# Recurrent down products one tile later, key-stage panels in halves, first queries loaded back early

## The reference

```python
# layer 0: gated recurrent mixer, 1536 channels
u = hn @ w_in; xb, yb = u[..., :1536], u[..., 1536:]
xc = causal_conv4(xb) + conv_b
r, i = sigmoid(blocks(xc, w_ra) + b_ra), sigmoid(blocks(xc, w_ix) + b_ix)
a = exp(-8 * r * softplus(-lam))
hs = scan(h_t = a_t * h_{t-1} + sqrt(1 - a_t**2) * i_t * xc_t)
h = h + (hs * gelu(yb)) @ w_out
# ... a gated feed-forward layer, then keys and values shared by the attention layer:
kv = rmsnorm(h) @ kv_w      # compressed, selected and window keys and values, 4 groups
kc, vc = gelu(windows(k_cmp) @ w1k) @ w2k, gelu(windows(v_cmp) @ w1v) @ w2v
# layer 1: 16 heads, three branches (compressed, selected, window), summed with gates
q = (hn @ w_q) * 96**-0.5   # 16 x 96, unrotated for kc, rotated for the other two
out = g0 * attend(q, kc, vc) + g1 * attend(rope(q), ks, vs) + g2 * attend(rope(q), kw, vw)
```

## Time and profile before

| | us |
|---|---|
| median of three runs (2611.04 to 2611.66) | 2611.09 |
| the profiled execution, its own time | 2616.25 |
| its span, first to last instruction | 2614.4 |
| TensorE busy in the span | 2440.1 |

### The profile page before, as it was taken

How to read it: one execution, slowest core, us unless ns; L and a number is a source line. 1 busy time by engine, 2 the same in 40 slices (tenths; PEclk the granted TensorE clock), 3 DMA queues, 4 the chain that set the end, 5 groups by cost and what they waited for, 6 DMA issues and landing times.

```text
span 2614.4 us, 28494 instructions
## 1 busy us (share of the span) xinstructions
PE 2440.1 (93%) x10912; PEld 1899.6 (73%) x10912; DVE 1406.2 (54%) x1711; ACT 1075.9 (41%) x1324; POOL 165.9 (6%) x140
## 2 busy tenths in 40 slices
PE   5999799999999979999999999899999889999958
PEld 4777678888778758887788888677787666666646
DVE  4666554444566645553544444556533556666654
ACT  3444443333333324452433333344422346666622
POOL 0333300000000000000000000300000000000020
PEclk9999899999999989999999999899999799999978
DMA  3222122222133431001222222011221239999941
GB/s 146 89 89 89 57 97 96 96 96 96 37 129 115 156 102 31 26 25 43 105 96 96 96 96 80 33 65 49 97 97 65 97 121 391 397 393 400 372 161 49
DMA packets 55808, 324.79 MB, mean 124 GB/s; under 512 B 6208, under 2 KB 6336, under 8 KB 25632
## 3 DMA queue, kind: packets, MB, share of 16 engines
q1 hardware_dynamic: 49072, 300.44, 30.5%
q0 software_dynamic: 5664, 20.84, 2.6%
q10 hardware_dynamic: 976, 2.21, 0.2%
HBM read 294.63 MB, written 28.84 MB: 124 GB/s over the span
## 4 chain that ended last, share of the span: by engine, by line
PE 83%; DVE 9%; ACT 3%; issue 2%; POOL 2%; DMA 1%; ACTq 0%; SPq 0%; POOLq 0%; DVEq 0%
PE psum L527 21%; PE psum L528 21%; PE psum L529 21%; PE psum L1159 5%; PE psum L899 3%; PE psum L846 3%; DVE a_lo L1695 2%; PE psum L863 1%; DVE tmp L1745 1%; PE psum L1121 1%; ACT a_hi L1204 1%; DVE hn_lo L1739 1%; PE psum L896 1%; PE psum L611 1%; DVE hs L1794 1%
## 5 line engine op out<-in xcount | busy, mean ns | idle before, releaser
L527 PE MATMUL psum<-hn_hi,a_hi 128*128 128x512 f32 (+2 forms) x1584 | 640.2, 404 | 33.9 <-DVE hn_lo L1739 20.0
L528 PE MATMUL psum<-hn_lo,a_hi 128*128 128x512 f32 (+2 forms) x1584 | 634.9, 401 | 0.0
L529 PE MATMUL psum<-hn_hi,a_lo 128*128 128x512 f32 (+2 forms) x1584 | 632.9, 400 | 0.0
L527 PEld LDWEIGHTS psum<-hn_hi,a_hi 128*128 128x128 f32 (+2 forms) x1584 | 299.4, 189 | 125.3 <-issue 23.4
L529 PEld LDWEIGHTS psum<-hn_hi,a_lo 128*128 128x128 f32 (+2 forms) x1584 | 298.9, 189 | 76.3 <-issue 0.8
L528 PEld LDWEIGHTS psum<-hn_lo,a_hi 128*128 128x128 f32 (+2 forms) x1584 | 299.6, 189 | 73.7 <-issue 1.0
L1695 DVE TENSOR_TENSOR a_lo<-a_raw,a_hi 128x2048 fp32r<-128x2048 f32 x117 | 271.1, 2318 | 113.4 <-ACT a_hi L1204 113.2
L1204 ACT ACTIVATE a_hi<-a_raw 128x2048 fp32r<-128x2048 f32 x117 | 223.1, 1908 | 134.7 <-PE psum L529 127.5
L2312 DVE TENSOR_TENSOR moe_lo<-moe_raw,moe_hi 128x2048 fp32r<-128x2048 f32 x78 | 178.7, 2292 | 43.7 <-ACT moe_hi L1622 43.3
L1781 DVE TENSOR_TENSOR h<-h,psum 128x512 f32<-128x512 f32 x176 | 121.1, 688 | 93.1 <-PE psum L529 91.6
L1622 ACT ACTIVATE moe_hi<-moe_raw 128x2048 fp32r<-128x2048 f32 x78 | 149.0, 1912 | 43.5 <-PE psum L529 26.5
(11 more groups left out here) (427 smaller groups left out, 3669.4 us busy)
## 6 DMA issues: line engine op xcount, KB each, us to landing
a_raw<-w_a SPq DMA_DIRECT2D x117, 1024.0 KB, 5.2
moe_raw<-w_m SPq DMA_DIRECT2D x78, 1024.0 KB, 9.0
moe_down<-w_m SPq DMA_DIRECT2D x39, 1024.0 KB, 8.3
b_raw<-w_b SPq DMA_DIRECT2D x64, 512.0 KB, 3.3
expert_out<-y_out SPq DMA_DIRECT2D x39, 512.0 KB, 8.5
q_scratch<-qb POOLq DMA_DIRECT2D x8, 768.0 KB, 5.3
qs<-q_scratch POOLq DMA_DIRECT2D x16, 384.0 KB, 3.6
out_t<-h POOLq DMA_DIRECT2D x8, 256.0 KB, 2.3
```

The lines of the kernel that those rows point to most:

```text
L527: pe.matmul(out, w_hi, x_hi, start=first, stop=False)
L528: pe.matmul(out, w_hi, x_lo, start=False, stop=False)
L529: return pe.matmul(out, w_lo, x_hi, start=False, stop=last)
```

## The change

Three places of the program change; no product is added or taken away.

1. In the recurrent layer, TensorE makes the tile `branch(g, 1, 0, ...)` ahead of `rnn_down(g - 1, 0)` rather than behind it. VectorE makes the low part of the gates' panel and the third convolution (with its `xc_lo`) ahead of `add_rnn(g - 1, 0)`, and ScalarE the third `high_xc` ahead of `high_b(B_RNN + 3g - 1)`.
2. The five panels of `HALVES` are rounded and split in two halves of 1024 columns; TensorE begins on the first half (`half_ready`) and waits for the whole panel ahead of the fifth of its eight slices. VectorE takes `low_a(A_W1V + 1)` ahead of four copies of values.
3. GpSimd loads heads 0 and 1 back when pair 1 has been stored, between the stores; ahead of head 2 it waits for all stores. `pt`, `pm` and `ptc` move over the b-buffers, so that `qs` no longer lies over `qb`. TensorE no longer waits for all rotations ahead of attention, and VectorE rotates the last pair behind `peak(0)`.

```diff
+HALVES = [A_K + 2, A_K + 4, A_K + 6, A_VCMP, A_W1V + 1]
...
             xv_lo = sb("xv_lo", [P, CSTRIDE, GROUPS * NCMP], F32R, st)
+        with ExitStack() as st:
+            sb("under_attention", [P, 3 * 2 * WA], F32, st)
+            pt = sb("pt", [P, 2, 2, S], F32, st)
+            pm = sb("pm", [P, 2, 2, S], F32, st)
+            ptc = sb("ptc", [NCMP, 2, S], F32, st)
...
             with ExitStack() as s2:
-                pt = sb("pt", [P, 2, 2, S], F32, s2)
-                ptc = sb("ptc", [NCMP, 2, S], F32, s2)
...
                 ob = sb("ob", [P, 2, 3, DV], F32, s2)
-                sb("under_pm", [P, P], F32, s2)
-                pm = sb("pm", [P, 2, 2, S], F32, s2)
+                sb("under_staged", [P, 7 * S], F32, s2)
...
+            def whole(s, n):
+                if s in HALVES:
+                    pe.wait_ge(half_ready, HALVES.index(s) + 1)
+                else:
+                    pe.wait_ge(a_ready, n + 1)
+            def rest(s, n, k):
+                if s in HALVES and k == KT // 2:
+                    pe.wait_ge(a_ready, n + 1)
...
                 n = s + 2 * i
-                pe.wait_ge(a_ready, n + 1)
+                whole(s, n)
+                def hh_rest(k):
+                    rest(s, n, k)
+                    return hh(k)
...
                     b = tile_bank(s, j, n)
-                    product(b[0:width, :], s, j * width, 2 * width, width, hh, hl).then_inc(tile_ready, 1)
+                    product(b[0:width, :], s, j * width, 2 * width, width, hh if j else hh_rest, hl) \
+                        .then_inc(tile_ready, 1)
...
                 branch(g, 0, 1, 1, f + 1)
+                branch(g, 1, 0, 2, f + 2)
...
                     rnn_down(g - 1, 0)
-                branch(g, 1, 0, 2, f + 2)
...
-            pe.wait_ge(rope_done, 8 + HEADS)
-            pe.wait_ge(tile_free, 2 * A_WO)
+            pe.wait_ge(rope_done, 8)
...
             scores_c(0)
+            pe.wait_ge(tile_free, 2 * A_WO)
...
                     act.wait_ge(tile_ready, 2 * n - 2)
-                act.activation(a_hi[s % 2][:, :], a_raw[s % 2][:, :], ACT.Copy).then_inc(a_rounded, 1)
+                if s in HALVES:
+                    act.activation(a_hi[s % 2][:, 0:WB], a_raw[s % 2][:, 0:WB], ACT.Copy).then_inc(half_rounded, 1)
+                    act.activation(a_hi[s % 2][:, WB:WA], a_raw[s % 2][:, WB:WA], ACT.Copy).then_inc(a_rounded, 1)
+                else:
+                    act.activation(a_hi[s % 2][:, :], a_raw[s % 2][:, :], ACT.Copy).then_inc(a_rounded, 1)
...
                     high_a(A_RNN + 4 * g + 2)
+                    high_xc(g, 2)
...
                 if g < RNN_GROUPS:
-                    high_xc(g, 2)
...
             expo(0)
-            for u in range(2):
-                act.wait_ge(q_stored[u], 16 * (HEADS // 4))
...
                 n = s + 2 * i
+                if s in HALVES:
+                    V.wait_ge(half_rounded, HALVES.index(s) + 1)
+                    V.tensor_tensor(a_lo[s % 2][:, 0:WB], a_raw[s % 2][:, 0:WB], a_hi[s % 2][:, 0:WB], ALU.subtract) \
+                     .then_inc(half_ready, 1)
+                    V.wait_ge(a_rounded, n + 1)
+                    V.tensor_tensor(a_lo[s % 2][:, WB:WA], a_raw[s % 2][:, WB:WA], a_hi[s % 2][:, WB:WA], ALU.subtract) \
+                     .then_inc(a_ready, 1)
+                    return
...
                     low_xc(g, 1)
-                if g:
-                    add_rnn(g - 1, 0)
-                if g < RNN_GROUPS:
                     low_a(A_RNN + 4 * g + 2)
-                if g:
-                    low_b(B_RNN + 3 * g - 1)
-                if g < RNN_GROUPS:
...
                 if g:
+                    add_rnn(g - 1, 0)
+                    low_b(B_RNN + 3 * g - 1)
...
             normalise(N_MIX1, 3)
+            low_a(A_W1V + 1)
...
             ins.then_inc(tile_free, 6)
-            low_a(A_W1V + 1)
...
             V.sem_inc(tile_free, 2)
+            def rotate_q(p):
+                for j in range(2):
+                    v = 2 * (p % 2) + j
+                    V.wait_ge(base_ready, 8 + 2 * p + j + 1)
+                    step(V.tensor_tensor(sq[0:ROT, j, :], qb[0:ROT, v, 0, :], cs[0:ROT, :], ALU.mult))
+                    V.wait_ge(tile_free, 2 * (A_Q + p) + j + 1)
+                    V.wait_ge(base_copied, 2 * p + j + 1)
+                    V.tensor_tensor(qb[0:ROT, v, 1, :], tmp[0:ROT, j, :], sq[0:ROT, j, :], ALU.add).then_inc(rope_done, 1)
...
                                            ALU.mult, ALU.mult).then_inc(tile_free, 1)
-                for j in range(2):
-                    v = 2 * (p % 2) + j
-                    V.wait_ge(base_ready, 8 + 2 * p + j + 1)
-                    step(V.tensor_tensor(sq[0:ROT, j, :], qb[0:ROT, v, 0, :], cs[0:ROT, :], ALU.mult))
-                    V.wait_ge(tile_free, 2 * s + j + 1)
-                    V.wait_ge(base_copied, 2 * p + j + 1)
-                    V.tensor_tensor(qb[0:ROT, v, 1, :], tmp[0:ROT, j, :], sq[0:ROT, j, :], ALU.add).then_inc(rope_done, 1)
+                if p < HEADS // 2 - 1:
+                    rotate_q(p)
...
                 V.wait_ge(o_ready, 3 * hd + 1 + 2 * half)
+                if hd == 0 and half == 0:
+                    for u in range(2):
+                        V.wait_ge(q_stored[u], 16 * (HEADS // 4))
...
             peak(0)
+            rotate_q(HEADS // 2 - 1)
...
                 store_q(p)
-            pool.wait_ge(q_stored[0], 16 * (HEADS // 4))
-            stage_q(0)
-            stage_q(1)
-            pool.wait_ge(q_stored[1], 16 * (HEADS // 4))
+                if p == 1:
+                    pool.wait_ge(q_stored[0], 16)
+                    pool.wait_ge(cmp_w2, 2)
+                    stage_q(0)
+                    stage_q(1)
+            for u in range(2):
+                pool.wait_ge(q_stored[u], 16 * (HEADS // 4))
```

More of the change, by code:

```diff
@@ L350, in build @@
             sem("m2_done"), sem("mult_done"), sem("bx_done"), sem("scan_done"), sem("rec_done"))
+        half_rounded, half_ready = sem("half_rounded"), sem("half_ready")
         base_ready, base_copied, rope_done = sem("base_ready"), sem("base_copied"), sem("rope_done")
@@ L750, in compress_v @@
                 s = A_W1V + p
-                pe.wait_ge(a_ready, s + 1)
+                whole(s, s)
                 if p == 0:
@@ L754, in compress_v @@
                 for l in range(8):
+                    rest(s, s, l)
                     t = 8 * p + l
```

## The result

| | before | after |
|---|---|---|
| median of four runs, us | 2611.07 (2610.36 to 2611.66) | 2567.49 (2566.72 to 2577.95) |
| the profiled execution, us | 2616.25 | 2567.22 |
| its span, us | 2614.4 | 2565.2 |

The ratio is 0.9843, with a 95% interval of 0.9817 to 0.9868: 43.6 us less. The forecast was 2568, in a range of 2562 to 2583.

The account below looks back on a forecast made before the run. TensorE, busy 93% of the span, bounds the kernel; time is won where it idles or runs at the lower clock. 11.8 + 5.2 + 6.3 + 2.9 + 2.1 + 12.0 + 3.0 = 43.3 us off 2611.09 gives 2568 us, range 2562 to 2583.

Parts of the forecast that it names:

- 11.8 of waits: Recurrent layer: the moved tile covers three of TensorE's four waits for the low part of `rhid`, 11.8 us.
- 5.2 of clock: Recurrent layer: the low clock behind the `rhid` waits goes with them, 5.2 us at most, nothing at least.
- what is late next: Recurrent layer, second down products: first addition and b-panel come 2.3 and 1.8 us early, so no new wait appears.
- Forecast 11.3 us: Panel halves: 6.3 us of four key-stage waits, 2.9 of low clock, 2.1 of the wait ahead of `compress_v(1)`.
- about 2.4 us were to stay: Ahead of `compress_v(1)`: the first half is ready 2.1 us sooner, and some 2.4 us of the wait stay.
- The allowance of 1.2 us: Halves: VectorE's queued copies may delay the first half, 0.3 us a panel, 1.2 in all, allowed in the range.
- The price of nothing for a wait within a product: Five split panels: a wait in the middle of a product costs nothing; otherwise the sum would be 0.9 us smaller.
- the row of FFN 0: FFN 0: one panel of two has a wait ahead of every slice, yet matmuls average 0.233 us.
- The 12.0 us of the wait: Start of attention: with heads 0 and 1 loaded after pair 1, `scores_c(0)` starts 12.0 us earlier.
- I take 3.0: First head of attention: full clock wins up to 7.6 us, less 4.2 of exposed VectorE work; 3.0 us taken.
- the clock falls in the ramp: Rival, start of attention: short waits lower the clock; queries give 7.8 instead of 15, total 32, 2579 us; chance 0.14.

Follow-up runs that it names:

- the last kernel: Changed kernel with the last pair's rotation behind `peak(1)` and the first group's panel 1 rounded and split ahead of the group loop: 2564.36 us, ratio 0.9813.
- TensorE's order alone: Kernel before with only TensorE's moved `branch(g, 1, 0, ...)` tile, VectorE and ScalarE as before: 2596.62 us, one execution.
- a wait in every slice: Changed kernel with a TensorE wait for a long-raised semaphore ahead of every triple of matmuls: 2569.0 us, one execution.
- the rotation last: Changed kernel with the last pair's rotation moved from behind `peak(0)` to behind `peak(1)`: 2567.69 us, ratio 0.9830.
- part 3 alone: Kernel before with only the early loading of queries: 2600.94 us, ratio 0.9956; second profile's execution 2603.35 us.
- part 2 alone: Kernel before with only the panel halves and `low_a(A_W1V + 1)` ahead of the copies: 2606.99 us, ratio 0.9982; second profile's execution 2602.66 us.

## Why the forecast held

**Recurrent layer: right.** Forecast 17.0 us (11.8 of waits, 5.2 of clock). Six profiles without the edit have a mean of 295.36 for the layer, the seven with it (the last kernel, which edits the layer further, left out) 277.72: 17.6 us. Timed alone the part gave 14.0, good to 3.4. The second down products came as reckoned: additions forecast to end at 116.9, measured 116.6; `b_lo` 118.1, measured 117.7; TensorE there at 117.1, measured 116.7. No new wait appeared. But the step "what is late next" reckoned with VectorE's new order as if it mattered, and with TensorE's order alone the layer is no longer.

**Halves: right.** Forecast 11.3 us. The key stage went from a mean of 136.6 to 125.1 in the profiles with the edit: 11.5. Of the wait ahead of `compress_v(1)` about 2.4 us were to stay, and 2.54 did. The allowance of 1.2 us for VectorE coming late was not needed: no wait for the first half shows ahead of `linear`. The price of nothing for a wait within a product holds too: the row of FFN 0 spoke for it, and a wait in every slice confirms it. So the Trainium skill's statement on weight loads taken ahead ("TensorE: Matmul & The Clock Gate", section "Architectural detail: the array is 16× 32×32, not 1× 128×128") meets no limit at a fulfilled wait that these runs can show.

**Queries: right in the wait, too small in the ramp.** The 12.0 us of the wait came whole (113.55 to 101.45, means). The term mis-sized is "I take 3.0" for the ramp. It stood for a full clock, worth 7.6 us, less 4.2 us of VectorE's work that TensorE waits for: 1.5 of the last copy and 2.7 of the rotation. Its stretch is that from `scores_c` of head 0 to head 1, which took 14.65 and 14.42 us in the two profiles of before and 10.16 and 10.17 after: 4.5 and 4.3 us won. The clock was full, and the work took what was reckoned. Head 1 on TensorE's timeline of before (after, it is at 918.97), then the window of the stretch after:

```profile
966.54 1.03 PE L836 MATMUL psum<-kct,qs 96*128 96x31 f32 x8
...
908.80:919.00 10.20, 7.67 (x44) 4.95 (x42) 7.59 (x14) 5.83 (x12) 0.63 (x1) 1.00 0.20 61
```

But TensorE waited only 0.69 us for the last copy (`tmp`), and of the rotation only 0.76 us reached it, by way of the second exponential (`pt`; with the rotation last this wait is gone): 1.45 us in place of 4.2. The third wait, of 1.08 us for `ptc`, is not the rotation's. It is as long with the rotation last, and most of it was there before. The waits list of before, then that with the rotation last:

```profile
PE psum L863 <- ACT ptc L1433: 0.8, 1, 0.8
...
PE psum L885 <- ACT ptc L1460: 1.1, 1, 1.1
```

Over the first three heads the times are 44.69 and 42.81 before and 38.32 after. Of the first profile's 6.4 us, 1.7 are a stretch at a lower clock between heads 2 and 3, which the second does not have (16.69 and 15.04 us).

**The sum: 43.3 forecast, 43.6 and 42.9 measured.** It agrees so closely partly by luck: the stages of the table fell by 17.6 + 11.5 + 12.1 + 5.4 = 46.6 us in their means. The first profile's stretches at the lower clock, from which the terms were taken, do not all repeat from one execution to the next, and waits that the change does not touch move as well: that of the norms for `sq` was 21.4 and 23.2 us before, 23.1 and 24.2 after.

**The rival "the clock falls in the ramp"** did not come true in the changed kernel's profiles: the granted clock was 1.00 throughout the ramp in both. (One of the four timed runs took 2577.95 us; what it did is not known.) With part 3 alone the rival came true, both times. The Trainium skill reports of another kernel that its clock went up and down because TensorE idled briefly and often between groups of matmuls ("TensorE: Matmul & The Clock Gate", section "A second HAM failure mode: psum-queue depth-cycling"). Part 3's fall to 0.63 among short waits is like it; the 1.00 of the whole change with the same waits is not.

The ramp's clock also accounts for a part of why the parts do not add up. In spans, two profiles each: part 1 (with TensorE's order alone) 2611.3 - 2595.5 = 15.8, part 2 8.6, part 3 11.4, together 35.8; the whole 44.8, 9.0 more. The ramp alone gains 5.4 us in the whole (43.8 to 38.3), but -1.2, -1.5 and 0.6 in the parts, -2.1 together: 7.5 of the 9.0 lie in it. Of these, part 3's 4.8 us less than the whole are shown to be the clock's, twice. The -1.2 and -1.5 of parts 1 and 2 are no more than chance, since their ramps have the program of before and part 2's two profiles differ by 8.4 us in it. Why the clock holds with all parts and falls with part 3 alone, where TensorE's program in the stretch is the same, was not found, and neither was the rest of the gap, which the timed medians put at 13 us.

## What to carry to other kernels

A wait for the end of a long chain is hidden by moving one independent tile of the same engine ahead of it; work out from the rows what then comes late, and try the order of that one engine first. Where a panel's preparation is the wait, begin on the first half of it; where a load is the wait, issue it as soon as its data lie in memory, even if buffers must move. Price the clock behind a wait apart from the wait, from several profiles, and test the parts together as well as alone.

## What the runs showed of the hardware

- The same program gave, from one execution to the next, other stretches at the lower clock: the first three heads took 49.42 and 41.00 us with part 2 alone, and behind the first group's wait for `rhid` the clock was 0.65 in one profile of before and 1.00 in the other.
- A wait of TensorE that is already fulfilled cost nothing measurable: 380.94 us for FFN 0 with one in every slice, 380.85 and 381.07 without.
- The same short waits in the ramp went with a granted clock of 1.00 in both profiles of the whole change, and of 0.60 and 0.63, in the 10.2 us from head 1 on, in the two of part 3 alone.
